# GpSimd forms the cosine difference of the spectral products too, in the jobs in which it has the sine sum already

## The reference, cut to what matters

```
def long_conv(z, h_freq):
    L = z.shape[1]
    zf = jnp.fft.rfft(z.astype(jnp.float32), n=2 * L, axis=1)
    return jnp.fft.irfft(zf * h_freq, n=2 * L, axis=1)[:, :L].astype(z.dtype)

    z = v
    for o, gate in enumerate((x1, x2)):
        z = gate * (long_conv(z, h_freq[:, o]) + flt_bias[o] * z)
```

## Time and profile before

| | us |
|---|---|
| median of 3 runs | 2652.79 (2649.28 to 2657.53) |
| the profiled execution's own time | 2653.97 |
| its span, first to last instruction | 2652.1 |
| PE busy | 2429.1 (92%) |
| DVE busy | 1072.5 (40%) |
| POOL busy | 689.5 (26%) |
| ACT busy | 620.8 (23%) |
| conv stage of layer 0 | 327 to 456 in the span |
| conv stage of layer 1 | 1644 to 1734 in the span |

### The profile page before, as it was taken

How to read it: one execution, slowest core, us unless ns; L and a number is a source line. 1 busy time by engine, 2 the same in 40 slices (tenths; PEclk the granted TensorE clock), 3 DMA queues, 4 the chain that set the end, 5 groups by cost and what they waited for, 6 DMA issues and landing times. The chain is left out here.

```text
span 2652.1 us, 35567 instructions
## 1 busy us (share of the span) xinstructions
PE 2429.1 (92%) x13080; PEld 1528.6 (58%) x13080; DVE 1072.5 (40%) x2132; ACT 620.8 (23%) x1371; POOL 689.5 (26%) x644
## 2 busy tenths in 40 slices
PE   8999988999999999998888899989999999998887
PEld 5455665455555555555555468645787555555553
DVE  5764477444222563211111175844432732222222
ACT  3441122443110232221111142234211311111111
POOL 0003122565221012222222222246431022222221
PEclk9999999999999999999999899999999999999999
DMA  9882030020212629999999913012125589999996
GB/s 365 352 344 103 14 108 19 13 55 7 65 48 87 237 109 390 396 400 401 403 390 386 350 51 117 32 32 55 48 72 204 233 337 394 393 405 405 403 405 245
DMA packets 191103, 588.29 MB, mean 222 GB/s; under 512 B 47424, under 2 KB 109163, under 8 KB 134668
## 3 DMA queue, kind: packets, MB, share of 16 engines
q1 hardware_dynamic: 166485, 551.86, 55.1%
q0 software_dynamic: 22400, 29.42, 3.4%
q10 hardware_dynamic: 2103, 5.51, 0.5%
HBM read 581.31 MB, written 51.51 MB: 239 GB/s over the span
## 5 line engine op out<-in xcount | busy, mean ns | idle before, releaser
L2634 PE MATMUL ps<-w,moe_xt 128*64 128x256 f32 x2816 | 337.5, 394 | 65.7 <-DMA w<-in_w_up_e 63.4
L2774 POOL DMA_INDIRECT rows_out<-moe_rows_out,table x128 | 117.7, 919 | 743.4 <-DVE moe_rows_out L2839 372.3
L2634 PEld LDWEIGHTS ps<-w,moe_xt 128*64 128x64 f32 x2816 | 220.5, 141 | 152.3 <-issue 67.7
L2889 DVE TENSOR_TENSOR moe_gated<-ps,moe_gated 64x256 f32<-64x256 f32 x128 | 54.5, 426 | 508.4 <-ACT moe_gated L2858 492.7
L2858 ACT ACTIVATE moe_gated<-ps 64x256 f32<-64x256 f32 x128 | 48.0, 375 | 670.2 <-PE ps L2634 562.2
L2634 PE MATMUL ps<-early_w,moe_xt 128*64 128x256 f32 x1280 | 154.2, 395 | 29.2 <-DMA early_w<-in_w_up_e 29.1
L1683 POOL TENSOR_SCALAR attn_p<-attn_p,attn_rs 128x768 f32<-128x768 f32 (+1 forms) x80 | 155.2, 1947 | 81.5 <-DVE attn_rs L1857 81.1
L2642 PE MATMUL ps<-w,moe_ht 128*64 128x512 f32 x704 | 171.3, 608 | 2.3 <-issue 2.3
L2155 PE MATMUL ps<-w_out,mix 128*128 128x512 f32 x320 | 144.6, 602 | 7.0 <-PEq L150 7.0
L2875 DVE TENSOR_TENSOR moe_rows_out<-ps,moe_row_gate 64x512 f32<-64x512 f32 x128 | 88.0, 688 | 138.5 <-PE ps L2642 136.4
L2634 PEld LDWEIGHTS ps<-early_w,moe_xt 128*64 128x64 f32 x1280 | 101.4, 142 | 68.1 <-issue 33.0
(11 more groups left out here) (432 smaller groups left out, 4291.1 us busy)
## 6 DMA issues: line engine op xcount, KB each, us to landing
w<-in_w_gate_e SPq DMA_DIRECT2D x88, 1024.0 KB
w<-in_w_up_e SPq DMA_DIRECT2D x88, 1024.0 KB
w<-in_w_down_e SPq DMA_DIRECT2D x88, 1024.0 KB
prep_w<-in_w_ada SPq DMA_DIRECT2D x24, 2048.0 KB, 16.3
early_w<-in_w_gate_e SPq DMA_DIRECT2D x40, 1024.0 KB
early_w<-in_w_up_e SPq DMA_DIRECT2D x40, 1024.0 KB
early_w<-in_w_down_e SPq DMA_DIRECT2D x40, 1024.0 KB
w_merge<-in_w_in SPq DMA_DIRECT2D x32, 512.0 KB, 5.3
```

The lines of the kernel that those rows point to most:

```text
L2634: last = nc.tensor.matmul(ps[k * SLOTS:(k + 1) * SLOTS, 0:DE], xt[:, c], wgu[:, k, c], start=c == 0, stop=c == KC - 1)
L2774: nc.gpsimd.indirect_dma_start(out=dram["y"], out_offset=bass.IndirectOffsetOnAxis(ap=m.table[0:SLOTS, j:j + 1], axis=0), in_=y[:, j % 2], ...
L2889: nc.vector.tensor_tensor(h[:, b % 2], m.ps[SLOTS:2 * SLOTS, b % 2, 0:DE], sg[SLOTS:2 * SLOTS, b % 2], ALU.mult).then_inc(s["h_done"], 1)
```

## The change

GpSimd gets a second operation per job of `pooled`: `cosine_sums(i)`, ahead of `sine_sums(i)`. It waits for the first two products of the job and forms the difference of `conv_t` in place. DVE no longer does so in these jobs; it waits for a new semaphore, `cosine_done`, at the place where its own subtraction stood. In the other jobs nothing changes.

```
+            def cosine_sums(i):
+                pool.wait_ge(s["products_done"], i + 1)
+                w = s["t"][:, :, 0:jobs[i][2] // P // 2]
+                nc.gpsimd.tensor_tensor(w[:, :, :, 0], w[:, :, :, 0], w[:, :, :, 1], ALU.subtract).then_inc(s["cosine_done"], 1)
...
                 if i in pooled:
+                    cosine_sums(i)
                     sine_sums(i)
...
                 dve.wait_ge(s["products_done"], i + 1)
                 dve.wait_ge(s["u_done"], i + 1)
-                if i not in pooled:
+                if i in pooled:
+                    dve.wait_ge(s["cosine_done"], pooled.index(i) + 1)
+                else:
                     nc.vector.tensor_tensor(u[:, :, :, 0], u[:, :, :, 0], u[:, :, :, 1], ALU.add)
-                link(nc.vector.tensor_tensor(w[:, :, :, 0], w[:, :, :, 0], w[:, :, :, 1], ALU.subtract))
+                    link(nc.vector.tensor_tensor(w[:, :, :, 0], w[:, :, :, 0], w[:, :, :, 1], ALU.subtract))
```

More of the change, by code:

```diff
@@ L1275, in conv_stage @@
     order0 = {(t, half): i for i, (t, _, _, o, half) in enumerate(jobs) if o == 0}
-    sems = ["dft1_in", "idft0_in", "idft1_in", "h1_in", "fwd_done", "other_done", "z_done", "z_joined", "products_done", "u_done", "sine_done", "dve", "y_done", "inv_done", "evac",
+    sems = ["dft1_in", "idft0_in", "idft1_in", "h1_in", "fwd_done", "other_done", "z_done", "z_joined", "products_done", "u_done", "cosine_done", "sine_done", "dve", "y_done", "inv_done", "evac",
             "latent_done", "sums_done", "halves_set", "var_done", "r_done", "scaled", "turned", "kept", "blank"]
```

## The result

The changed kernel takes 2658.71 us in the median of 16 runs (2650.95 to 2663.62), the one before 2652.64 (2649.28 to 2657.53): a ratio of 1.0019, interval 1.0012 to 1.0027, so 3 to 7 us slower, 5.0 at 1.0019 (the two medians by themselves lie 6.1 apart). The direction and the bound of 0.3% were as forecast; the size was +1.3 in the forecast and +5.0 as measured. The profiled execution took 2654.42 us with a span of 2652.6. The two conv stages are 4.1 us longer in its trace (3.28 and 0.78), and the unchanged rest of the program happened to be 3.6 us shorter.

The account below looks back on a forecast made before the run. No engine is full; VectorE and TensorE wait on each other, so VectorE time counts in latent jobs. Per-job gains and losses summed to +1.3 us, 2655.3 profiled, so a median of 2654.1 us, range 2647.5 to 2661.

Parts of the forecast that it names:

- the sum of the collisions: Gains and losses per job in both conv stages, GpSimd holding VectorE up against the saved subtraction: +1.3 us, chance 0.70.
- if the granted clock of an inverse changes: Sign against the forecast: in the changed kernel's profile, TensorE's granted clock over an inverse differs from before.
- A microsecond on VectorE counts in the latent jobs and not in the context jobs: Conv stages: TensorE waits for VectorE in latent jobs, VectorE for TensorE in context jobs; five savings of 1.24 us count.
- The collision: Second pair of products: a GpSimd operation of 2.36 us reading SBUF holds a two-SBUF-input VectorE instruction back 2.15 us.
- Job 0: Layer 0: no collision in the pair, sine sum holds the first sum to 346.82; gain 0.5 us.
- job 1: Layer 0: the difference gets between the pair's two instructions, costing 2.15 us against 1.24 saved; loss 0.9 us.
- job 5: Layer 0: the 2.15 us hold-up, with only 0.18 us of wait behind it and 1.24 saved; loss 0.7 us.
- layer 1: Its job 0: the difference holds back the pair by 2.15 us against 1.24 saved; loss 0.9 us.
- Job 4: Layer 0: hold-up hidden by a wait for ScalarE, 1.24 us saved, half a microsecond lost to slower roots; gain 0.7 us.
- TensorE's gaps: Idle before the inverse of job 4 shorter by about 0.7 us, before those of jobs 1 and 5 longer by as much.
- The clock as a rival: TensorE's clock falls in the longer gap (3.3 us) before job 5's inverse: 2.5 us more, 2656.6, up to 2664; chance 0.13.
- The engines don't disturb each other: GpSimd doesn't slow VectorE in the conv stages, so all five savings count: 6.2 us, 2646.6 us; chance 0.12.
- the difference is late: VectorE waits outright for GpSimd's difference, some 1 us in each of three jobs: 2657 us; chance 0.05.

Follow-up runs that it names:

- the filled kernels: The kernel before and the changed kernel, each with unread identity matmuls that end inside TensorE's gaps: ratios to the unfilled kernel before 1.0001 and 0.9997.
- the latent jobs alone: Against the kernel before, GpSimd forms the difference only in the five latent jobs, VectorE in the context jobs: 2657.23 us, ratio 1.0018.

## Why the prediction was right, and where its size was off

The time lies in the stated range, and that is in part luck. The forecast value was the sum of the collisions, which lies 4.6 us below the median; the range had been widened for the clock falling once or twice, and it fell. By the prediction's own signs the forecast is wrong "if the granted clock of an inverse changes", and three did by more than 0.05: that of job 5 from 1.00 to 0.67, that of job 4 from 0.59 to 0.67, that of job 0 of layer 1 from 1.00 to 0.67.

- *A microsecond on VectorE counts in the latent jobs and not in the context jobs.* Half right, and the step that failed. The context jobs do wait for TensorE, but job 3's saving isn't nothing. It brings the inverse of job 3 forward by 0.3 us against the projections. It also makes the roots of latent 7 0.5 us longer (1.02 + 1.52 in place of 0.61 + 1.40), for VectorE's instructions that read SBUF twice now lie otherwise: the first root instruction ends 0.07 us behind the end of such an instruction in both traces (397.85 before, 396.81 after). Together TensorE's gap grows by 0.86. The 0.5 was in the sum, in job 4; what followed from the gap was not.
- *The collision.* 2.16 us measured, 2.15 predicted. The rule of the Trainium skill (SBUF — State Buffer, Who interferes with whom) holds, with 2.16 in place of the whole 2.36.
- *Job by job, at L1546 or the inverse.* Each figure is what the job adds, counted from the stage's start. Job 0 -0.6 (forecast -0.5); job 1 +0.9 (+0.9); job 5 +0.6 (+0.7); layer 1 +0.8 (+0.9). Job 4 was forecast at -0.7 and came out at +1.0; less the forward transform's 1.68 at low clock that is -0.7. So VectorE's and GpSimd's part came out nearly as forecast: added up by jobs +0.9, against +1.3. (At the ends of the stages 0.8 of it is left.) Of TensorE's gaps one sign was wrong: that before the inverse of job 1 became shorter (2.28 us, before 2.70), since the late roots put 1.10 us of idle time ahead of the transposes before it. That before job 4 became shorter, as forecast (2.82, before 4.08).
- *The clock as a rival, 0.13.* It took place, in the inverse of job 5 as described (+1.63 and not 2.5, behind a gap of 4.04 and not 3.3), and also in the forward transform, a place I had not looked at. The forecast of 0.70 for the collisions alone was too sure: of the trace's 4.1 over both stages they make 0.8 and the clock 3.3. That the clock carries the loss is shown by the filled kernels, where the changed one and the one before take the same time (2650.31 and 2650.34). The fills stand in both layers, so they show this of all the low stretches together. That the single falls are worth 1.68 and 1.63 is read from one trace and its repetition. It isn't the whole account of the median either: the latent jobs alone lose as much as the changed kernel (1.0018), with neither of the two falls of layer 0 in their trace, and why stays open.
- *The engines don't disturb each other; the difference is late.* Neither was seen: VectorE waited for `cosine_done` in no job of the changed kernel.

## What to carry to other kernels

Work moved from VectorE to GpSimd was free here beside VectorE instructions that read PSUM; beside those with two SBUF inputs it cost VectorE nearly GpSimd's whole time (2.16 of 2.36 us), so look in the trace at what the moved instruction will lie next to, not at how idle GpSimd is. Where TensorE waits often and briefly, an edit that is worth nothing by its own sum can lengthen a gap by less than a microsecond (0.86 here) and cost more than that through the granted clock (1.68). List every gap that the edit lengthens, those behind a third engine too, and price the work behind each at the low clock.

## What the runs showed of the hardware that I had not expected

A TensorE gap of 2.66 us left the clock full once and low once in the same kernel. Ahead of the inverse of job 0 of layer 1, a gap of 2.30 to 2.33 us left it full in five traces and low in four, and the four have 0.66 to 0.82 us of idle time ahead of the transposes right before: the length of the last gap by itself doesn't tell. Fills of the gaps restored the full clock, but faster matmuls alone made the next gap longer, and the low clock moved there (5.47 us behind a fill that ended 2.5 us early).
